# A decoder layer with 64 routed experts: the last group's results are summed to tokens by one-hot products, and the first two sorted groups get smaller shapes

## What is computed

```python
def moe_ffn(h, router_w, router_bias, e_gate, e_up, e_down, s_gate, s_up, s_down):
    ...
    _, idx = lax.top_k(jnp.where(expert_mask, biased, -jnp.inf), TOP_K)
    w = jnp.take_along_axis(scores, idx, axis=1)
    w = w / jnp.sum(w, axis=-1, keepdims=True) * ROUTED_SCALE
    gates = jnp.zeros((n, N_EXPERTS), jnp.float32).at[jnp.arange(n)[:, None], idx].set(w)
    hg = jnp.einsum('nd,edf->nef', h, e_gate)
    hu = jnp.einsum('nd,edf->nef', h, e_up)
    act = jax.nn.silu(hg) * hu * gates[:, :, None].astype(h.dtype)
    routed = jnp.einsum('nef,efd->nd', act, e_down)
    shared = (jax.nn.silu(h @ s_gate) * (h @ s_up)) @ s_down
    return routed + shared
```

## Time and profile before

| | us |
|---|---|
| median of 3 runs | 976.56 |
| lowest and highest | 975.34, 980.02 |
| the profiled execution's own time | 976.05 |
| its span in the trace | 974.3 |
| granted TensorE clock, mean | 0.954 |

### The profile page before, as it was taken

How to read it: one execution, slowest core, us unless ns; L and a number is a source line. 1 busy time by engine, 2 the same in 40 slices (tenths; PEclk the granted TensorE clock), 3 DMA queues, 4 the chain that set the end, 5 groups by cost and what they waited for, 6 DMA issues and landing times.

```text
span 974.3 us, 20651 instructions
## 1 busy us (share of the span) xinstructions
PE 857.8 (88%) x7579; PEld 626.5 (64%) x7579; DVE 466.9 (48%) x1252; ACT 273.1 (28%) x521; POOL 170.9 (18%) x178
## 2 busy tenths in 40 slices
PE   3799999999998999899989998987988888889880
PEld 2699999999998987446545554644545555455440
DVE  2657889899968564323334432322323322222224
ACT  4644444443374220112112121211211221112122
POOL 2000000000000001122232323323232222322211
PEclk9899999999999989999989999999998999999995
DMA  9974557888876439789999999999999999999942
GB/s 329 307 243 145 175 175 283 281 270 282 274 275 230 134 151 417 273 278 347 379 380 389 397 384 402 395 394 391 398 400 383 407 385 390 391 392 391 389 148 94
DMA packets 99850, 305.65 MB, mean 314 GB/s; under 512 B 11459, under 2 KB 51459, under 8 KB 74796
## 3 DMA queue, kind: packets, MB, share of 16 engines
q1 hardware_dynamic: 87275, 281.63, 76.3%
q0 software_dynamic: 12016, 21.78, 8.4%
q10 hardware_dynamic: 499, 1.40, 0.4%
HBM read 301.86 MB, written 21.97 MB: 332 GB/s over the span
## 4 chain that ended last, share of the span: by engine, by line
PE 49%; DMA 41%; DVE 5%; issue 3%; ACT 1%; SPq 1%; POOLq 0%; DVEq 0%; ACTq 0%
DMA wexp<-in_e_up 34%; PE psum L771 25%; PE psum L1042 5%; PE psum L1039 5%; PE psum L775 4%; DMA y_even<-mT,scatter_row 3%; PE psum L790 2%; PE psum L1079 2%; DMA wexp<-in_ada_w 1%; DMA wexp<-in_w_in 1%; PE psum L958 1%; PE psum L1011 1%; DMA xn<-h_table,idx 1%; PE psum L1044 1%; PE psum L1084 1%
## 5 line engine op out<-in xcount | busy, mean ns | idle before, releaser
L771 PE MATMUL psum<-xn_r,wexp_r 128*128 128x264 f32 x1024 | 192.4, 288 | 3.0 <-DVE wexp_r L1472 2.4
L771 PEld LDWEIGHTS psum<-xn_r,wexp_r 128*128 128x128 f32 x1024 | 161.0, 191 | 4.4 <-DVE wexp_r L1472 3.6
L694 POOL DMA_INDIRECT y_even<-mT,scatter_row x64 | 92.7, 1448 | 389.0 <-DVE gcol L1856 108.2
L1042 PE MATMUL psum<-wexp,mid 128*128 128x512 f32 x304 | 141.1, 610 | 13.1 <-DMA wexp<-in_e_up 12.3
L771 PE MATMUL psum<-hT_r,wexp_r 128*128 128x264 f32 x512 | 146.0, 285 | 0.0
L1890 DVE SCALAR_TENSOR_TENSOR hT<-psum,gcol,hT 128x256 f32<-128x256 f32 (+1 forms) x64 | 26.6, 415 | 245.8 <-ACT hT L1378 245.8
L1472 DVE TENSOR_TENSOR wexp_r<-wexp,wexp_r 128x1024 fp32r<-128x1024 f32 x88 | 106.3, 1217 | 24.0 <-ACT wexp_r L1222 23.8
L1222 ACT ACTIVATE wexp_r<-wexp 128x1024 fp32r<-128x1024 f32 x88 | 92.2, 1054 | 52.0 <-PE psum L771 41.4
L1039 PE MATMUL psum<-wexp,mid 128*32 128x128 f32 x1920 | 77.5, 304 | 31.0 <-DMA wexp<-in_e_up 30.8
L1042 PEld LDWEIGHTS psum<-wexp,mid 128*128 128x128 f32 x304 | 56.0, 194 | 75.3 <-issue 74.1
L771 PEld LDWEIGHTS psum<-hT_r,wexp_r 128*128 128x128 f32 x512 | 97.6, 191 | 0.1
(11 more groups left out here) (294 smaller groups left out, 1060.7 us busy)
## 6 DMA issues: line engine op xcount, KB each, us to landing
wexp<-in_e_gate SPq DMA_DIRECT2D x64, 1024.0 KB
wexp<-in_e_up SPq DMA_DIRECT2D x64, 1024.0 KB
wexp<-in_e_down SPq DMA_DIRECT2D x64, 1024.0 KB
wexp<-in_w_in SPq DMA_DIRECT2D x32, 1024.0 KB, 6.2
mid<-in_ada_w SPq DMA_DIRECT2D x8, 2048.0 KB, 9.8
wexp<-in_ada_w SPq DMA_DIRECT2D x4, 2048.0 KB, 20.4
wexp<-in_w_branch SPq DMA_DIRECT2D x8, 1024.0 KB, 5.6
wexp<-in_w_out SPq DMA_DIRECT2D x4, 1024.0 KB, 5.7
```

The source lines that it names most:

```text
L694: g.indirect_dma_start(out=y_even, out_offset=bass.IndirectOffsetOnAxis(ap=scatter_row[0:n, j, :].bitcast(mybir.dt.uint32), axis=0), in_=y ...
L771: last = mm(out, a[x], b[y], start=start and x == y == 0, stop=stop and x == 1)
L1042: last = mm(psum[:, j % 2, :].rearrange("p (a f) -> p a f", a=2), x[:, k, :], w[:, k], start=(k == 0), stop=(k == KT - 1))
```

## The change

1. In group 0, the list of job (1,0) is made on PE inside `up` of job (0,1), behind six of its eight steps and the turn of job (0,0), where it stood right behind `sort`.
2. Groups 1 and 2 (`LIGHT_GROUPS`) get the shapes 32, 64, 32, 64. The ranks are dealt anew: in groups 3 to 15 the 128-row jobs take ranks 4 to 16 and the 64-row jobs 17 to 29, the light groups' 64-row jobs 30 to 33, the 32-row jobs ranks 34 to 63, with the last four in the light groups.
3. The four jobs of group 15 aren't scattered. Their results lie in SBUF twice: gated (`y_rows`, DVE's `gated_out`) for the prompt tokens and raw (`raw_rows`, ACT's `raw_out`) for the sample tokens, job 60 in part 0, jobs 61 to 63 in part 1. DVE makes one-hots from the lists (`to_token`), and PE sums the rows to tokens in PSUM (`last_sum`): part 0 under and behind job 63, part 1 at the end.
4. POOL, not SP, loads `fin_y`, when the scatters of groups 0 to 14 have landed and job 61's `up` is done. DVE adds the two large tiles to `x_sb` in job (15,2) (`add_table`); the sample tile comes into PSUM by a product with the identity.
5. The extra passes come last and use `y_odd`, which is zeroed with `y_even` at the beginning. The length of the longest list is read by each engine before group 15.

```diff
+LIGHT_GROUPS = 2
+FULL_GROUPS = GROUPS - LIGHT_GROUPS
 ROWS_OF_JOB = (CAP, QUARTER, HALF, QUARTER)
-LARGE = FIXED + GROUPS
+ROWS_OF_LIGHT_JOB = (QUARTER, HALF, QUARTER, HALF)
+LARGE = FIXED + FULL_GROUPS
+OVER_QUARTER = LARGE + FULL_GROUPS + 2 * LIGHT_GROUPS
 SHARED_FROM = 3
 RANK_SCALE = float(1 << 20)
+LAST = NE // UNROLL - 1
+SCATTERED = NE - UNROLL
+LAST_ROWS_AT = (0, 0, HALF, QUARTER)
+LAST_BANKS = ((5, 6), (0, 1))
+SAMPLE_BANK = LIST_BANK
+SAMPLE_TILE = 32
...
+            if isinstance(i, int) and i == 0:
+                return CAP
+            return (ROWS_OF_LIGHT_JOB if isinstance(i, int) and i <= LIGHT_GROUPS else ROWS_OF_JOB)[j]
...
-            for table in (y_even,):
+            for table in (y_even, y_odd):
...
-                t0, n = TILES[t]
-                sp.dma_start(fin_y[0:n, t], y_even[t0:t0 + n]).then_inc(fin_ld[t], 16)
+            extra_passes(sp, longest_list(sp), extra, finish=load_added)
...
-            sp.wait_ge(S["moe_done"], 1)
-            sp.wait_ge(S["scattered"], 16 * NE)
-            for t in FINAL_ORDER:
-                t0, n = TILES[t]
-                sp.dma_start(fin_y[0:n, t], y_even[t0:t0 + n]).then_inc(fin_ld[t], 16)
...
-            g.iota(ranks[:, :, 0:4:2], pattern=[[1, GROUPS], [GROUPS, 2]], base=FIXED, channel_multiplier=0)
-            g.iota(ranks[:, :, 1:4:2], pattern=[[2, GROUPS], [1, 2]], base=FIXED + 2 * GROUPS, channel_multiplier=0)
+            light, full_ = ranks[:, 0:LIGHT_GROUPS, :], ranks[:, LIGHT_GROUPS:, :]
+            g.iota(full_[:, :, 0:4:2], pattern=[[1, FULL_GROUPS], [FULL_GROUPS, 2]], base=FIXED, channel_multiplier=0)
...
+            await_full(pool, ("shared_up", 1))
+            g.iota(token_order.bitcast(I32), pattern=[[1, TOK]], base=0, channel_multiplier=0).then_inc(S["tokens_in"], 1)
             def body(i, first=False, last=False):
                 for j in range(UNROLL):
-                    if not (first and j == 0):
+                    if not (first and j == 0) and not (last and j):
...
-            scatter(NE // UNROLL - 1, UNROLL - 1)
-
-            def all_scattered():
-                pool.wait_ge(S["scattered"], 16 * NE)
+            pool.wait_ge(S["scattered"], 16 * SCATTERED)
+            pool.wait_ge(S["up_done"], UNROLL * LAST + 2)
+            for t in FINAL_ORDER:
+                t0, n = TILES[t]
+                g.dma_start(fin_y[0:n, t], y_even[t0:t0 + n]).then_inc(fin_ld[t], 16)
...
+            def last_sum(a, t, h, first=False):
+                t0, n = TILES[t]
+                out = psum[SAMPLE_TILE * h:SAMPLE_TILE * h + n, SAMPLE_BANK, :] if t == 2 else psum[:, LAST_BANKS[t][h], :]
+                y = raw_rows if t == 2 else y_rows
+                return mm(out, to_token[:, a, t0:t0 + n], y[:, a, h * BLK:(h + 1) * BLK], start=first, stop=(a == 1),
+                          tile_position=(0, SAMPLE_TILE * h if t == 2 else 0))
+            def rows_ready(jobs):
+                pe.wait_ge(S["ys_act"], jobs)
+                pe.wait_ge(S["ys_dve"], jobs)
+            def first_sums_of_large():
+                rows_ready(UNROLL * LAST + 1)
+                pe.wait_ge(S["to_token_ready"], 1)
+                pe.wait_ge(S["xgt_act"], NE)
+                pe.wait_ge(S["xgt_dve"], NE)
+                for h in range(2):
+                    last_sum(0, 0, h, first=True)
+                pe.wait_ge(S["lst_ready"], NE)
+                for h in range(2):
+                    last_sum(0, 2, h, first=True)
+            def last_sums():
+                pe.wait_ge(S["act_ready"], NE - 1)
+                last_sum(0, 1, 0, first=True)
+                turn_act(LAST, UNROLL - 1)
+                down(LAST, UNROLL - 1)
+                pe.wait_ge(S["act_ready"], NE)
+                last_sum(0, 1, 1, first=True)
+                pe.wait_ge(fin_ld[2], 16)
+                for h in range(2):
+                    mm(psum[SAMPLE_TILE * h:SAMPLE_TILE * h + NS, SAMPLE_BANK, :], ident[0:NS, 0:NS], fin_y[0:NS, 2, h * BLK:(h + 1) * BLK],
+                       start=False, stop=False, tile_position=(0, SAMPLE_TILE * h))
+                rows_ready(NE)
+                pe.wait_ge(S["to_token_ready"], 2)
+                for t in FINAL_ORDER:
+                    for h in range(2):
+                        last_sum(1, t, h).then_inc(S["last_sum"], 1)
...
-                    up(i, j, (0, 1, 2, 3))
+                    late = first and j == 1
+                    up(i, j, range(6) if late else range(4))
...
-                    up(i, j, (4, 5, 6, 7))
+                    if late:
+                        token_list(i + 1, 0)
+                    up(i, j, range(6, KT) if late else range(4, KT))
...
-                    if not last:
+                    if not last and prev:
                         token_list(i + 1, j)
                     if shared_piece_at(i, j) is not None:
                         shared_down(shared_piece_at(i, j))
+                    if last and j == 2:
+                        first_sums_of_large()
...
+            def raw_out(j):
+                e = UNROLL * LAST + j
+                n, a, rows = rows_used(LAST, j), min(j, 1), rows_of_last(j)
+                ac.wait_ge(S["down_done"], 2 * e + 1)
+                if n == QUARTER:
+                    for q in range(4):
+                        if q == 2:
+                            last.then_inc(S["bank3_copied"], 1)
+                            ac.wait_ge(S["down_done"], 2 * e + 2)
+                            ac.wait_ge(S["bank4_gated"], j + 1)
+                        last = F(raw_rows[rows, a, q * FE:(q + 1) * FE], psum[q * n:(q + 1) * n, 3 + q // 2, 0:FE], ACT.Copy)
+                else:
+                    F(raw_rows[rows, a, 0:BLK], psum[CAP - n:CAP, 3, :], ACT.Copy).then_inc(S["bank3_copied"], 1)
+                    ac.wait_ge(S["down_done"], 2 * e + 2)
+                    ac.wait_ge(S["bank4_gated"], j + 1)
+                    last = F(raw_rows[rows, a, BLK:D], psum[0:n, 4, :], ACT.Copy)
+                last.then_inc(S["ys_act"], 1)
...
+            def gated_out(j):
+                e = UNROLL * LAST + j
+                n, a, rows = rows_used(LAST, j), min(j, 1), rows_of_last(j)
+                ve.wait_ge(S["down_done"], 2 * e + 2)
+                ve.wait_ge(S["scattered"], 16 * min(e - 1, SCATTERED))
+                def gate(c0, c1, p0, bank):
+                    return V.tensor_tensor(y_rows[rows, a, c0:c1], psum[p0:p0 + n, bank, 0:c1 - c0], bc[p0:p0 + n, 3, c0:c1], ALU.mult)
+                if n == QUARTER:
+                    for q in (2, 3):
+                        last = gate(q * FE, (q + 1) * FE, q * n, 4)
+                else:
+                    last = gate(BLK, D, 0, 4)
+                last.then_inc(S["bank4_gated"], 1)
+                ve.wait_ge(S["bank3_copied"], j + 1)
+                if n == QUARTER:
+                    for q in (0, 1):
+                        last = gate(q * FE, (q + 1) * FE, q * n, 3)
+                else:
+                    last = gate(0, BLK, CAP - n, 3)
+                last.then_inc(S["ys_dve"], 1)
+            def rows_to_tokens():
+                ve.wait_ge(S["lst_ready"], NE)
+                V.tensor_copy(token_of[:, 0:1], idx[:, 0, :])
+                for j in range(1, UNROLL):
+                    rows = rows_of_last(j)
+                    at = rows.start % HALF
+                    last = V.tensor_copy(token_of[rows, 1:2], idx[at:at + rows_used(LAST, j), j, :])
+                link(last)
+                for a in range(2):
+                    V.tensor_scalar(to_token[:, a, :], token_order, token_of[:, a:a + 1], None, ALU.is_equal).then_inc(S["to_token_ready"], 1)
+            def add_table(t):
+                n = TILES[t][1]
+                ve.wait_ge(fin_ld[t], 16)
+                link(V.tensor_tensor(fin_y[0:n, t], fin_y[0:n, t], rows_of(3, t, n, 0, D), ALU.mult))
+                mark(V.tensor_tensor(x_sb[0:n, t, :], x_sb[0:n, t, :], fin_y[0:n, t], ALU.add))
...
+                    if last and j == 2:
+                        add_table(0)
+                        add_table(1)
...
+            ve.wait_ge(S["dve_chain"], n_chain[0])
+            for m, t in enumerate(FINAL_ORDER):
                 n = TILES[t][1]
-                ve.wait_ge(fin_ld[t], 16)
-                link(V.tensor_tensor(fin_y[0:n, t], fin_y[0:n, t], rows_of(3, t, n, 0, D), ALU.mult))
-                V.tensor_tensor(x_sb[0:n, t, :], x_sb[0:n, t, :], fin_y[0:n, t], ALU.add).then_inc(S["fin_red"], 1)
+                for h in range(2):
+                    a = slice(h * BLK, (h + 1) * BLK)
+                    ve.wait_ge(S["last_sum"], 2 * m + h + 1)
+                    if t == 2:
+                        p0 = SAMPLE_TILE * h
+                        last = V.tensor_tensor(fin_y[0:n, t, a], psum[p0:p0 + n, SAMPLE_BANK, :], rows_of(3, t, n, a.start, a.stop), ALU.mult)
+                    else:
```

(7 more changed lines are left out.)

91 lines of the change are left out of this document (61 added, 30 removed).

## The result

| | median | of before | 95% interval |
|---|---|---|---|
| before, same session | 976.27 us (8 runs) | 1 | |
| changed | 970.85 us (966.68 to 974.16, 8 runs) | 0.9941 | 0.9922 to 0.9960 |
| forecast | 966.1 us | 0.9893 | |

So the change gains 5.4 us by the medians (5.8 by the ratio), where 10.5 was forecast. One of the twelve executions of e3_tail, an experiment further down, took 2788.55 us at a mean granted clock of 0.295, and is left out of what is said of that kernel.

The account below looks back on a forecast made before the run. Bound by weight loading on DMA, with holes in the first group and a serial tail; -6.1 (list) + 2.0 (light shapes) - 7.6 (tail) + 1.2 (table) = -10.5 us from 976.56, so 966.1 us, range 961.5 to 972.5.

Parts of the forecast that it names:

- What bounds the kernel: Whole kernel: DMA with holes from 395 to 435 us, then full weight loading, then a serial tail of 31.6 us.
- The list, -6.1: Group 0: moving the first sorted list removes PE's 4.52 us wait and slow steps, so weights start 6.1 us earlier.
- The rival in which the engines that end last had no hole: Front: its gain isn't passed on, as the last DMA engines were busy in the holes; 970.2 us, chance 0.15.
- Light shapes, +2.0: Groups 1 and 2: 156 rows (0.64 MB) move into the stage with full DMA, costing 2.0 us, bounds 0 and 2.4.
- Zeroing, 0: Start: SP's zeroing of the second table ends by 330, before SP's next issue at 336.46; cost 0, uncovered up to 9.
- The tail, -7.6: From job 61's down product to the end: products replace the last scatters and table load, ending at 966.7, -7.6 us.
- The price of the table, +1.2: Tail: loading the table among the last weights and adding it on DVE before job 63's gating costs 1.2 us.
- the forecast's sign for a table in time: Tail: DVE's wait for the table was to be under 3 us.
- the late table: Tail rival: the table lands late and holds DVE ahead of job 63's gating; +4 us, 970.1 to 972, chance 0.08.
- the lower clock: Tail rival: the products run at TensorE's lower clock; +5 us, 971.1, chance 0.12.
- the 2.7 of that sum: Tail: by the skill's queue section, 1.08 MB of table delays the last weights by 2.7 us; sum -9.0, 967.6 us.
- Slower by the DMA engines' load: Expert loop rival: changed row order loads the slowest DMA engine with 15 us more work; 982 us, chance 0.03.

Follow-up runs that it names:

- e3_tail: The changed kernel with the list in its old place and no light groups, so the new tail alone: 973.91 us, ratio 0.9974 to before.
- e1_list: The kernel before with only the first sorted list moved: 970.23 us against 976.78, ratio 0.9928.
- e5_best: The changed kernel without light groups, so moved list and new tail: 969.02 us against 975.46 before, ratio 0.9919.
- e4_light: The kernel before with the light groups alone: 979.41 us, ratio 1.0023 to before.
- e8_pool: e5_best with the two large table tiles multiplied and added on GpSimd, not VectorE: 963.38 us, ratio 0.9867 to before.
- e10_after_pool: The changed kernel, light groups included, with the two large table tiles multiplied and added on GpSimd: 965.86 us, ratio 0.9884 to before.
- e12_filler: e5_best with three unused products on TensorE ahead of the last turn, the product there put behind it: 966.10 us, ratio 0.9900 to before.
- e7_none: e5_best without the table's load, multiply and add (that part of the result missing): 963.13 us against 976.85 before, ratio 0.9855.
- e2_front: The kernel before with the list moved and the light groups, old tail kept: 973.60 us, ratio 0.9969 to before.
- e6_split: e5_best with the second large table tile multiplied and added behind job 63's gating on VectorE: 965.23 us, ratio 0.9896 to before.

## Right and wrong, step by step

**What bounds the kernel: right.** Three stages, with the holes of the first group worth their time and the tail serial. In the middle the light groups left PE idle for 3.75 us out of 5 while the DMA share stayed at 1.01.

**The list, -6.1: right, for the stated reason.** PE's idle and its slow steps are gone, the reload moved by 4.8 us in an execution whose sort ended 1.1 later, that is by 5.9. The middle stretch shrank by 549.1 - 542.9 = 6.2 us over seven kernels; the runs of e1_list say 6.6 to 7.0. The rival in which the engines that end last had no hole has fallen.

**Light shapes, +2.0: sign right, a little small.** Measured 2.5 on average of four pairings, 2.5 and 2.8 by the stretches, just beyond the upper bound of 2.4. The rows moved as forecast. Counted from 5 to 33 us behind the sort product's end, which is 396.6 to 424.6 in e5_best (first line) and 397.6 to 425.6 in the changed kernel (second line), the software queue has:

```profile
q0 software_dynamic: 560, 0.96, 12.2%
q0 software_dynamic: 464, 0.32, 6.0%
```

It is 0.96 MB in all seven kernels with the moved list alone and 0.32 in all three that have light groups too; beside the old list, 43 us from the sort product's end, it is 1.01 MB in before and e3_tail and 0.37 in e4_light. The difference of 0.64 MB is the forecast's own. Its price by the earlier trace rows, 2.4 us, is an estimate close to the measured 2.5. That these bytes cost the time, and not the new order of the ranks that comes with them, no run separates.

**Zeroing, 0: right.** The changed kernel's SP queue:

```profile
320.61 4.62 SPq L537 DMA_DIRECT2D y_odd<-zeros  x2
336.46 0.33 SPq L541 DMA_DIRECT2D mod_room<-in_s_down  x1
```

The cover holds; the next issue stands at 336.46, as in the earlier trace rows.

**The tail, -7.6: right where nothing held it.** Its sum gave 26.15 us; e8_pool has 26.4, e10_after_pool 26.95. The products take 0.9 us a slot (3.70 for four calls), and from the last down product to the end it is 15.9 us, as forecast.

**The price of the table, +1.2: the step that failed.** It was the term with the widest bounds (-1.2 to +6). e8_pool against e5_best gives 5.1 us by the ratios and 5.6 by the medians; e10_after_pool against the changed kernel 5.6 by either. So it was some 5.4 where 1.2 stood, without the 0 to 2 us of the load itself, which these kernels keep; those 4.2, with 0.5 more for the light groups, make up 4.7 of the 5.1 us by which the forecast missed. The working had VectorE free "at 947.5 to 949.5", which is 7.0 to 9.0 us behind the end of job 61's down product on the clock of before (940.55). The profiles have 9.3 (changed, 946.93 less 937.63), 9.6 (e12_filler), 9.7 (e3_tail) and 10.2 (e5_best), so the table was later than the latest that the working allowed for. Three things follow. First, the hold: 1.3 us in the changed kernel's profile and 2.4 to 2.8 in the others. The working had only the turn wait for it, not ScalarE's copy behind it. Second, TensorE's two idle times, before the turn and before the down product, stand close together, and in e5_best and e3_tail the clock then fell to 1.2 GHz under the products that the change had put there (3.5 and 4.0 us). Third, the forecast's sign for a table in time, a wait of VectorE under 3 us, was met (1.29 + 1.18 us) although the hold was there; how late job 63's gating comes is what counts. I had the late table and the lower clock as two separate rivals, +4 and +5 us with 0.08 and 0.12. They are one: the late table makes the idle, and without the idle (e12_filler, e8_pool, e10_after_pool) the clock held. With a price for each by itself, neither could be the likeliest.

The measured 970.85 us lies inside the range of 961.5 to 972.5, near its upper end, but beside the number of a rival that has fallen: 970.2, the front's gain lost. By its time alone one would have picked the wrong cause.

The profile of the changed kernel doesn't show the second part, because in that execution the clock held; its time of 968.04 was the second lowest of eight. Its three stretches against before (+1.1, -4.1, -5.4) make -8.4, the median is -5.4. If the clock costs 3.5 to 4.0 us whenever it falls, then the price of 5.6 less a hold of 1.3 to 2.8 leaves 2.8 to 4.3 for it, which would mean that it fell in most executions. That is an estimate: the traces show one such execution each of e3_tail and e5_best, and how often it happened to the changed kernel was not seen.

**The table's landing.** It was slow, as the earlier trace rows had let one fear: the three table loads were issued at 931.92 and VectorE began with the first tile at 940.74 and with the second at 944.41.

```profile
931.92 1.75 POOL L756 DMA_DIRECT2D wexp<-y_even  x3 [5.72 <-DMA y_even<-mT,scatter_row]
```

That fits the section on queues, rings and completion order of the Trainium skill's page "DMA: Bandwidth & Descriptors", by which the table's packets share each engine with the weights'. But the weights hardly paid for it: job 63's came without a wait in the changed kernel, and the load's price by e7_none is 0 to 2 us, not clearly the 2.7 of that sum.

**Slower by the DMA engines' load: did not happen at that size.** The middle stretch is 4.1 us shorter than before, not 15 longer. A small effect of this kind isn't excluded: the new order of the ranks comes with the light groups, and their 2.5 to 2.8 us may hold some of it.

## To carry to other kernels

A load that is to be hidden under the last work must not be consumed by an in-order engine ahead of something that this work waits for; give the consumption to an idle engine, here GpSimd, even if it is half as fast. When work is put on TensorE at the end of a chain, look at every idle time ahead of it together, since together they may be followed by the lower clock under all that comes next; an idle and its clock are to be priced as one case. Cutting single executions at two fixed points told effects of 2 to 6 us apart that the spread of whole runs (7 us) nearly hid.

## What the runs showed of the hardware

- Two waits of 1.2 to 2.2 and 1.3 us in a row in the tail were followed by 8 us at a granted clock of 0.50, though PE was busy throughout those 8 us (4.00 of 4 in both windows; e3_tail, e5_best). Waits of 0.93, 0.30 and 1.31 us were not (changed), but waits of 0.55 and 1.04 us were followed by some 3 us at 0.50 (e6_split). A single wait of 2.14 us was followed by a granted clock of 0.82 (before), one of 1.97 us by 1.00 (e2_front). So the length of a wait alone doesn't tell here whether the clock falls. Four products of 512 columns take 3.70 us at 2.4 GHz; one takes 2.08 at 1.2 GHz against 1.12.
- GpSimd multiplies or adds 128x1024 fp32 in 2.35 us, VectorE in 1.23. VectorE's gating at the same time was not slowed (1.41 us for two pieces of 64x512, with and without it).
- The profiled execution need not be a typical one: a clock that falls in some executions and not in others is seen only when several kernels with the same tail are compared.
